# Sparse-attention trunk on one core: index layout by a TensorE product, threshold search in steps of four bits

## The reference

```python
s = einsum('bqhd,bsd->bqhs', qi, ki) * IDX_DIM**-0.5
score = einsum('bqhs,bqh->bqs', relu(s), wi * IDX_HEADS**-0.5)
score = where(kpos <= qpos, score, -inf)
_, idx = top_k(score, topk)          # sample group: the best 256 of 2049 positions, per request
phys = page_table[idx // PAGE_SIZE]; off = idx % PAGE_SIZE
ks, vs = cache_k[phys, off], cache_v[phys, off]   # or the new key and value
out = softmax(q . ks * HEAD_DIM**-0.5) . vs
```

## Time and profile before

| | |
|---|---|
| median of 3 runs | 1848.12 us (1846.99 to 1849.04) |
| span of the profiled execution | 1859.2 us (its own time is given by this span alone) |
| mean granted TensorE clock | 0.987 |
| PE busy | 1785.8 us, 96% |
| DVE busy | 1455.6 us, 78% |
| ACT busy | 932.3 us, 50% |
| POOL busy | 423.1 us, 23% |

### The profile page before, as it was taken

The page is one execution under the profiler, slowest core; times in us unless marked ns, Lnnn a source line. Parts: engine busy times, 40 slices in busy tenths (PEclk is TensorE's granted clock), DMA queues, the critical chain, the costliest instruction groups (busy, mean ns, idle before and its releaser), DMA issues.

```text
span 1859.2 us, 35839 instructions
## 1 busy us (share of the span) xinstructions
PE 1785.8 (96%) x14076; PEld 1701.5 (92%) x14076; DVE 1455.6 (78%) x2186; ACT 932.3 (50%) x1464; POOL 423.1 (23%) x312
## 2 busy tenths in 40 slices
PE   7999999999999699999999999999999899999997
PEld 7999999987965478999999989999999799999996
DVE  5988886676978327988888689888866988887875
ACT  4455562353357535655563374555633465556433
POOL 3100044271220336100044230000442320002430
PEclk9999999999999899999999999999999999999998
DMA  5563323236110233244332323433233124433231
GB/s 166 190 203 91 112 86 103 87 108 146 38 54 1 52 108 91 69 113 111 92 114 80 105 74 106 112 91 113 86 103 110 44 69 113 113 92 112 80 103 47
DMA packets 277680, 180.73 MB, mean 97 GB/s; under 512 B 11574, under 2 KB 274110, under 8 KB 277053
## 3 DMA queue, kind: packets, MB, share of 16 engines
q1 hardware_dynamic: 268279, 158.52, 29.9%
q0 software_dynamic: 2144, 13.04, 2.0%
q10 hardware_dynamic: 7150, 7.68, 1.7%
HBM read 169.55 MB, written 8.08 MB: 96 GB/s over the span
## 4 chain that ended last, share of the span: by engine, by line
PE 75%; DVE 14%; ACT 5%; issue 3%; DMA 1%; POOL 0%; SPq 0%; ACTq 0%; DVEq 0%; POOLq 0%
PE ps L1373 40%; PE ps L1252 15%; PE ps L1436 9%; PE ps L1496 2%; DVE w_lo L1957 2%; PE ps L1712 2%; PE ps L1501 1%; DVE q_lo L2640 1%; ACT xf L753 1%; ACT xh L751 1%; ACT p_t L888 1%; DVE w_lo L2533 1%; PE ps L1273 1%; DVE q_sum L2717 1%; ACT sc L866 1%
## 5 line engine op out<-in xcount | busy, mean ns | idle before, releaser
L2804 POOL TENSOR_TENSOR hl<-hid_all,hh 128x520 fp32r<-128x520 f32 x56 | 98.1, 1785 | 748.8 <-ACT hh L1112 748.8
L1042 ACT CAST w_hi<-w_sum 128x1024 fp32r<-128x1024 f32 x160 | 168.0, 1050 | 114.6 <-DVE w_sum L2515 107.1
L2533 DVE TENSOR_TENSOR w_lo<-w_sum,w_hi 128x1024 fp32r<-128x1024 f32 x160 | 194.5, 1218 | 4.5 <-ACT w_hi L1042 4.5
L1252 PE MATMUL ps<-hh,w_hi 128*128 128x260 f32 x896 | 191.7, 284 | 2.0 <-DVE w_lo L1957 2.0
L1252 PE MATMUL ps<-hh,w_lo 128*128 128x260 f32 x896 | 189.2, 282 | 0.0
L1373 PE MATMUL ps<-t_hi,w_hi 128*128 128x260 f32 x640 | 161.6, 284 | 0.7 <-DVE w_lo L2533 0.5
L1373 PE MATMUL ps<-t_hi,w_lo 128*128 128x260 f32 x640 | 160.7, 283 | 0.0
L1373 PE MATMUL ps<-xh,w_hi 128*128 128x260 f32 x640 | 159.9, 282 | 0.8 <-DVE w_lo L2533 0.8
L1373 PE MATMUL ps<-xh,w_lo 128*128 128x260 f32 x640 | 159.5, 283 | 0.0
L1252 PEld LDWEIGHTS ps<-hh,w_hi 128*128 128x128 f32 x896 | 145.4, 188 | 3.0 <-issue 2.7
L1252 PEld LDWEIGHTS ps<-hh,w_lo 128*128 128x128 f32 x896 | 145.6, 188 | 0.2
(11 more groups left out here) (372 smaller groups left out, 5264.2 us busy)
## 6 DMA issues: line engine op xcount, KB each, us to landing
w_raw<-in_ffn_wi_dram SPq DMA_DIRECT2D x176, 512.0 KB
w_raw<-in_ffn_wo_dram SPq DMA_DIRECT2D x16, 1024.0 KB
w_raw<-in_ffn_wo_dram SPq DMA_DIRECT2D x32, 512.0 KB
w_raw<-in_ffn_wo_dram SPq DMA_DIRECT2D x16, 768.0 KB
w_raw<-in_attn_w_in_dram SPq DMA_DIRECT2D x8, 1024.0 KB
keys_scratch<-key_half POOLq DMA_DIRECT2D x2, 2048.0 KB, 8.6
w_raw<-in_attn_w_o_dram SPq DMA_DIRECT2D x4, 1024.0 KB
x_in<-in_x_prompt_dram ACTq DMA_DIRECT2D x4, 512.0 KB, 10.2
```

Of the source, the lines that this page charges most:

```text
L1042: nc.scalar.copy(blocks(st, j)[1][0][:, x], w_sum[:, c % 2, x]).then_inc(s_sums_hi, 1)
L1252: mm = nc.tensor.matmul(ps[0:mc, bank + 2 * m + h, 0:HT], w[:, k, m, 0:mc], x(k)[:, h * HT:(h + 1) * HT], start=first and k == 0 and w is ...
L2533: nc.vector.tensor_tensor(lo[:, x], w_sum[:, (st.chunk + j) % 2, x], hi[:, x].bitcast(F32), ALU.subtract).then_inc(s_sums_lo, 1)
L2804: nc.gpsimd.tensor_tensor(hl[:, k, :], hid_all[:, k, :], hh[:, k, :].bitcast(F32), ALU.subtract).then_inc(s_hl, 1)
```

## The change

Two edits. The search takes 8 steps of four bits (the last of three) with 15 candidates in place of 11 steps with 7. And the indices no longer pass through DRAM: DVE spreads idx_f over 128 columns by multiplying it with a constant, one PE product with a second constant puts each index at its place, and DVE copies the result into idx_sb. With it the 32 gathers are issued in one go in POOL's block 8 (GATHERS = {8: 4 * DEC}), the semaphore s_idx now says that idx_sb is written, and SP's two small DMAs wait for s_slots, which PE raises after L1682. The side steps on DVE are now 0 to 14, those on PE 0 to 13 with one empty place before step 12.

```diff
-STEPS = (28, 25, 22, 19, 16, 13, 10, 7, 4, 1, 0)
+STEPS = (27, 23, 19, 15, 11, 7, 3, 0)
+CANDS = 15
 UNITS_OF = len(STEPS)
...
+    digit, request = p[:, None] // DEC, p[:, None] % DEC
+    out["spread"] = (digit % 8 == np.arange(8)[None, :])
+    col = np.arange(2 * DEC)[None, :]
+    out["place"] = (request == col // 2) & (digit // 8 == col % 2)
...
-        tests = at("tests", [P, NC + 1, DEC, 7], BF16)
+        tests = at("tests", [P, NC + 1, DEC, CANDS], BF16)
...
-        GATHERS = {8: 2, 9: 4, 10: 4, 11: 4, 12: 4, 13: 4, 14: 4}
+        GATHERS = {8: 4 * DEC}
...
-                sp.wait_ge(s_idx, 1)
-                sp.dma_start(idx_dram.rearrange("b (h l) -> h b l", l=16), idx_f[:]).then_inc(s_idxd, 16)
                 sp.wait_ge(s_kvo, 16 * 6)
+                sp.wait_ge(s_slots, 1)
                 for dst, n in ((k_sel, 6), (v_sel, 7)):
...
-                sp.wait_ge(s_idxd, 16)
-                sp.dma_start(idx_sb[:], idx_dram.rearrange("b (t p) -> p (b t)", p=P), allow_slow_non_contiguous=True)\
-                  .then_inc(s_idxl, 16)
...
-                                mm = nc.tensor.matmul(ps[:, 6, 0:DEC * 7 * 3], ones_bf[:],
+                                mm = nc.tensor.matmul(ps[:, 6, 0:DEC * CANDS * 3], ones_bf[:],
...
+                    if n == SIDES + 1:
+                        pe.wait_ge(s_wide, 1)
+                        nc.tensor.matmul(ps[:, 6, 0:2 * DEC], idx_wide[:].rearrange("p h l -> p (h l)"), cst("place"),
+                                         start=True, stop=True).then_inc(s_placed, 1)
...
-                steps = iter([*range(SIDES), None, SIDES])
+                steps = iter([*range(SIDES), None, SIDES, SIDES + 1])
...
-                    widths = 7 if STEPS[k] else 1
+                    widths = CANDS if STEPS[k] else 7
...
-                        nc.vector.scalar_tensor_tensor(idx_f[:], slots[:, 0, :], float(PAGE), slots[:, 1, :],
-                                                       ALU.mult, ALU.add).then_inc(s_idx, 1)
+                        done(step(nc.vector.scalar_tensor_tensor(idx_f[:], slots[:, 0, :], float(PAGE), slots[:, 1, :],
+                                                                 ALU.mult, ALU.add)))
+                        nc.vector.tensor_tensor(idx_wide[:], idx_f[:].unsqueeze(1).broadcast_to([P, 8, 16]),
+                                                cst("spread").unsqueeze(2).broadcast_to([P, 8, 16]), ALU.mult).then_inc(s_wide, 1)
+                        dve.wait_ge(s_placed, 1)
+                        nc.vector.tensor_copy(idx_sb[:], ps[:, 6, 0:2 * DEC]).then_inc(s_idx, 1)
...
-                        pool.wait_ge(s_idxl, 16)
+                        pool.wait_ge(s_idx, 1)
```

More of the change, by code:

```diff
@@ L68 @@
 for _name, _n in (("ident", P), ("mean", P), ("dup0", P), ("dup1", P), ("tri", P), ("ones8", P), ("cap", P),
-                  ("causal", P), ("edge", 64), ("iota", 16), ("unit", UNITS_OF * 7), ("kv_of", 4), ("own", DEC), ("parity", 2), ("token", 1)):
+                  ("causal", P), ("edge", 64), ("iota", 16), ("unit", UNITS_OF * CANDS), ("kv_of", 4), ("own", DEC), ("parity", 2), ("token", 1),
+                  ("spread", DEC), ("place", 2 * DEC)):
     CONST[_name] = (CONST_COLS, _n)
@@ L87, in constants @@
     out["iota"] = np.tile(np.arange(16.0), (P, 1))
-    unit = np.array([[j << u if u or j == 1 else 0 for j in range(1, 8)] for u in STEPS], np.int32).reshape(1, -1)
+    unit = np.array([[j << u if u or j < 8 else 0 for j in range(1, CANDS + 1)] for u in STEPS], np.int32).reshape(1, -1)
     out["unit"] = np.tile(unit.view(np.float32), (P, 1))
@@ L264, in trunk_kernel @@
         top[0] = silu_off
-        idx_f = at("idx_f", [P, 16], I32)
+        idx_f = at("idx_f", [P, 16])
+        idx_wide = at("idx_wide", [P, 8, 16])
         found = at("found", [P, 32, DEC])
@@ L275, in trunk_kernel @@
         top[0] = kidx_off
-        tests = at("tests", [P, NC + 1, DEC, 7], BF16)
+        tests = at("tests", [P, NC + 1, DEC, CANDS], BF16)
         hits = at("hits", [P, DEC, NC], BF16)
         thr = at("thr", [P, DEC], I32)
-        cand = at("cand", [P, DEC, 7], I32)
+        cand = at("cand", [P, DEC, CANDS], I32)
         delta = at("delta", [P, DEC], I32)
-        reach = at("reach", [P, DEC, 7])
+        reach = at("reach", [P, DEC, CANDS])
         need = at("need", [P, DEC])
@@ L313, in trunk_kernel @@
         keys_dram = nc.dram_tensor("keys_scratch", [DEC * N_PAGES, 2, PAGE // 2 * IDX_DIM], F32, kind="Internal").ap()
-        idx_dram = nc.dram_tensor("idx_scratch", [DEC, 256], I32, kind="Internal").ap()
         def halves(x):
@@ L439, in trunk_kernel @@
         s_idx = sem("s_idx")
-        s_idxd = sem("s_idxd")
-        s_idxl = sem("s_idxl")
+        s_wide = sem("s_wide")
+        s_placed = sem("s_placed")
         s_newkv = sem("s_newkv")
@@ L2196, in test @@
                 def test(k):
-                    units = cst("unit")[:, 7 * k:7 * k + 7].bitcast(I32)
-                    n = step(nc.vector.tensor_tensor(cand[:], thr[:].unsqueeze(2).broadcast_to([P, DEC, 7]),
-                                                     units.unsqueeze(1).broadcast_to([P, DEC, 7]), ALU.bitwise_xor))
+                    units = cst("unit")[:, CANDS * k:CANDS * k + CANDS].bitcast(I32)
+                    n = step(nc.vector.tensor_tensor(cand[:], thr[:].unsqueeze(2).broadcast_to([P, DEC, CANDS]),
+                                                     units.unsqueeze(1).broadcast_to([P, DEC, CANDS]), ALU.bitwise_xor))
                     done(n)
-                    nc.vector.tensor_tensor(tests[:], score[:].rearrange("p b n -> p n b").unsqueeze(3).broadcast_to([P, NC + 1, DEC, 7]),
-                                            cand[:].bitcast(F32).unsqueeze(1).broadcast_to([P, NC + 1, DEC, 7]), ALU.is_ge)\
+                    nc.vector.tensor_tensor(tests[:], score[:].rearrange("p b n -> p n b").unsqueeze(3).broadcast_to([P, NC + 1, DEC, CANDS]),
+                                            cand[:].bitcast(F32).unsqueeze(1).broadcast_to([P, NC + 1, DEC, CANDS]), ALU.is_ge)\
                       .then_inc(s_hits, 1)
                 def take(k):
-                    widths = 7 if STEPS[k] else 1
+                    widths = CANDS if STEPS[k] else 7
                     dve.wait_ge(s_cnt, k + 2)
-                    at_ = step(nc.vector.tensor_reduce(reach[:], ps[:, 6, 0:DEC * 7 * 3].rearrange("p (x b j) -> p b j x", b=DEC, j=7),
+                    at_ = step(nc.vector.tensor_reduce(reach[:], ps[:, 6, 0:DEC * CANDS * 3].rearrange("p (x b j) -> p b j x", b=DEC, j=CANDS),
                                                        AX.X, ALU.add))
@@ L2216, in take @@
                     done(at_)
-                    at_ = step(nc.vector.tensor_tensor(delta[:], need[:], cst("unit")[:, 7 * k:7 * k + 1].bitcast(I32).broadcast_to([P, DEC]),
+                    at_ = step(nc.vector.tensor_tensor(delta[:], need[:], cst("unit")[:, CANDS * k:CANDS * k + 1].bitcast(I32).broadcast_to([P, DEC]),
                                                        ALU.mult))
```

## The result

The change made the kernel slower. The median is 1861.81 us (four runs, 1859.92 to 1862.09) against 1848.58 for the kernel before beside it (1846.99 to 1849.29): ratio 1.0075, interval 1.0063 to 1.0087, so +13.2 us. The prediction had the sign and the place, but 1855.8 and an upper end of 1860: the cost was 13.2 us in place of 7.7.

A forecast was written before the change was run, and what follows sets the result against it. No engine bounds the attention as a whole, but DVE is nearly full in blocks 2 to 5. Block 12 starts 7.7 us later, the layout gives 0, so 1848.1 + 7.7 = 1855.8 us; range 1847 to 1860.

The forecast's parts named there:

- main case: Whole kernel: +7.7 us, with a size from +5 to +10; chance 0.62.
- The side step, +1.60: DVE's search: each full step of take and test grows by 1.60 us, to 4.21 us.
- Rival 1, the cheap test: DVE's search: wider tests run at the bf16 rate, a full step +0.5, so no change, 1847 to 1848; chance 0.11.
- The first test: The search's first test on DVE, ahead of block 2: +1.27 us, moving block 2's start by as much.
- DVE's waits of 2.6 us in these blocks are swallowed: Blocks 2 to 5: the longer DVE work absorbs all its waits there, a credit of 2.6 us.
- The small blocks: Blocks 6, 7 and 9: lengths of 7.65, 9.0 and 5.85 us.
- Block 8, 8.9 us: Block 8: slot products in 2.03 us, then DVE's stand for the placing product and second row maxima; 8.9 us in all.
- rival 3: Blocks 7 and 8: PE's waits for s_hot bring its clock down, +3 us on top, 1858.8; chance 0.14.
- The search is over three steps sooner: From block 6 on: the search ends earlier, which gives back 1.0 us in blocks 7 to 11.
- The layout at 0: Index path: the 7 us DRAM trip goes and gathers come earlier, worth 0 us because nobody waited for them.
- The accident of the first profile: Blocks 12 and 13: 12.6 us too long in that profiled run only, so the sum starts from the median.
- Rival 2: Blocks 12 and 13: their stand comes from the gathers in timed runs too, and goes: -4.9 us, 1843.2; chance 0.13.

The follow-up runs named there:

- search-only kernel: The changed kernel with the old DRAM index layout and paced gathers put back, keeping the eight four-bit steps: 1860.86 us, ratio 1.0074.
- filler kernel: The changed kernel plus 44 useless PE products before the wait for the one-hot matrices in block 7: 1859.48 us, ratio 1.0069.
- late-copy kernel: The changed kernel with DVE's copy of idx_sb, and its wait, one side step later: 1862.78 us, ratio 1.0082.
- the layout alone: The changed kernel with the old eleven three-bit steps, keeping the new index layout and gathers: 1846.22 us, ratio 0.9994.
- the wide spread: The changed kernel with the late copy and its one-hot and index steps at most one to a block: 1859.17 us, ratio 1.0069.
- the narrow spread: The changed kernel with eleven narrow steps, late copy, last side steps one to a block and gathers in block 10: 1856.60 us, ratio 1.0050.
- the narrow search: The changed kernel with 7 candidates a step in place of 15, still 8 steps, so it picks other positions: 1850.26 us, ratio 1.0014.
- with two: The kernel with 44 filler products plus 36 more on PE before the second wait for tests: 1861.33 us, ratio 1.0067.

## Why the prediction was wrong in size

Two steps of the prediction failed. It gave back DVE's 2.6 us of waits in blocks 2 to 5 as swallowed, where 1.2 us were. And its main case ran PE at full clock through block 8, with the low clock as a rival of chance 0.14, where the low clock came in both profiles of the changed kernel and cost 2.7 us, the largest single term of the miss. The side step itself was sized well. Step by step, against the second trace of the changed kernel and the repeat of the kernel before:

- **The side step, +1.60: right.** Tests took 2.41 us (2.41 forecast), the reduction 0.53 (0.53), cand 0.28 (0.29), the full step 4.18 (4.21). Rival 1, the cheap test, is excluded. The first test made block 1 longer by 1.15 us (1.27).
- **"DVE's waits of 2.6 us in these blocks are swallowed": this step failed.** The added work without that credit was 9.60 + 1.2 = 10.8; blocks 2 to 5 grew by 47.61 - 38.05 = 9.56, so 1.24 was swallowed, and 1.3 us of waits are still there. The waits for xh, 2.2 us over four places in the earlier trace rows, fell to 0.6, the one at the end of block 5, and there a new one stands ahead of it: row_inv waits 0.5 for ACT's exponentials. Both come right after the last take, where DVE has nothing long left to do. In the first profile, with the clock low in block 2, PE's products came late too (reach, 1.5 us), and 2.6 us of waits stood again. The forecast gave the whole of a wait back because another engine would have time to catch up; it named no trace row for that.
- **The small blocks.** Block 6 took 8.13 us for 7.65 forecast: its model was a block with fewer of the search's counting products, and PE is busy 7.88 of the 8.13 us. Block 9 took 6.31 for 5.85: it was taken for a block without a remainder, and PE is busy 5.72 us in it for the 4.57 of the earlier trace rows. Together +0.9. Block 7 took 8.83 for 9.0.
- **Block 8, 8.9 us: near at full clock, wrong as run. This step failed too, and by more.** With PE kept busy it takes 9.33, in the search-only kernel 9.11; in the changed kernel 12.03 and 12.09. The missing 2.7 us are rival 3, the low clock around the slot products. It was priced rightly (+3) and given 0.14, when the longer wait before them (2.58 us, 1.41 before) was one that the forecast itself had derived. It is no rival of the main case but a term on top of it, and not a sure one: of five profiles with a wait of 2.57 or 2.58 us there, four have the low clock behind it and one, the search-only kernel's, has not. That 8.9 came so near is in part luck, since the forecast reached it through DVE's stand (see the layout below).
- **The sum.** Against the forecast's block table: -0.1 for block 2's start, +1.5 for blocks 2 to 5, +0.5 in block 6, -0.2 in block 7, +3.2 in block 8 (2.7 of it clock), +0.5 in block 9 make +5.4, so 7.7 becomes 13.1. Measured in the blocks +12.95, timed +13.2.
- **"The search is over three steps sooner":** the forecast gave blocks 7 to 11 back 1.0 us for that. At full clock they give 0.3 (36.2 us in the filler kernel, 36.4 before), and with the clock as it is they cost 2.5.
- **The layout at 0: right** (ratio 0.9994), for the reason given. DVE's stand of 3.34 us (2 to 3 forecast) was seen, but the forecast chained block 8 through it; the late-copy kernel shows that, at the low clock, the chain runs PE, ACT, PE beside it. The first gather was forecast at 616 and came at 620.2, at the late end of block 8; nobody waited for it. (By their distance of 1.30 us the issues from 616 on would end at 635.5 and 656.3, not at 637 and 658; nothing hangs on it.)
- **The accident of the first profile: right.** Rival 2 is excluded: blocks 12 and 13 take 6.76 and 7.14 in the repeat of the kernel before, and its median is no lower.

What stays open is what decides where the clock is low. A wait of PE goes before it, but no length of wait in these traces settles it. Before the slot products, a wait of 1.41 or 1.42 us was followed by full clock in four profiles (both of the kernel before, the layout alone, the wide spread), one of 1.87 by the low clock (the narrow spread), and one of 2.57 or 2.58 by the low clock in four (three of them the changed kernel with or without the late copy, the fourth the narrow search) and by full clock in one (the search alone). In block 13 PE waits 1.62 or 1.63 us ahead of the same products in the repeats of both kernels and in the wide spread, at full clock, and in the filler and the search-only kernel, at 0.81. Nor does the low clock of block 13 stand in for that of block 8: the narrow kernel has both, the wide spread neither. Each profile is one execution, so how often a kernel's runs have it isn't on record.

The Trainium skill ("TensorE: Matmul & The Clock Gate", What's actually happening) says that the throttled state is the default and activity lifts it. The trace agrees where filler products replace the wait in block 8 (clock 1.00 for 0.77), but the search-only kernel had 1.00 there without them.

## What to carry to other kernels

A search with wider digits trades steps for candidates: here 8 steps of 15 cost 4.2 us each where 11 of 7 cost 2.6, on an engine that was already nearly full in those blocks, while the steps saved lay in blocks whose length another loop set. Before you credit a wait as absorbed, ask which engine would have to come earlier; if it also got more work, or its own input comes from the late one, keep the wait in the sum. And when a forecast itself makes PE wait longer before a dense row of products, give the half clock for that row its price and a real chance in the main case; here it came in four profiles of five with that wait.

## What the runs showed of the hardware

- **The half clock comes and goes behind the same wait.** PE waited 2.58 us ahead of the same 17 products in the changed and in the search-only kernel; they took 3.81 us at 0.50 in one, 2.03 at 1.00 in the other.
- **A low stretch costs about 1.5 to 3 us wherever it falls:** in block 8 of the changed kernel (12.09 for 9.33), or in block 13 with one filler, with two, in the search-only kernel and in the two narrow variants (8.75 to 8.81 for 7.14). It is absent from both blocks in the wide spread.
- **One execution can carry 12.5 us of its own.** In the first profile of the kernel before, blocks 12 and 13 took 26.37 us; in every later profile of any version, 13.9 to 15.7.
- **The time of a run is its span plus 1.8 to 2.0 us** in all that have both (1847.82 and 1846.0, 1859.92 and 1858.1, 1861.91 and 1860.1). The Trainium skill ("Runtime: NRT & Kernel Launch", The ~15µs preamble/postamble breakdown) puts a profile's total about 6 us above the reported time; no run here shows that. With 1.8 us added, the first profiled execution comes to about 1861.0 (an estimate from these rows), 12.9 above the median, and its two long blocks hold 12.5 of that.
